# Hyena's inverse transform by even and odd times, around the first tiles of the output product; router and experts asked for apart

## The reference, cut to what matters

```python
p = h @ w_in                                  # 1024 -> 3 * 1024
p = sum(pp[:, j:j + L] * conv_w[j] for j in range(3)) + conv_b
x0, x1, v = jnp.split(p, 3, axis=-1)
z = v * x1
z = irfft(rfft(z, 2L) * rfft(circ, 2L))[:L] + bias * z      # circ: the normed filter, both directions
y = x0 * z
return y @ w_out
# then x = x + g1 * mix; h = modulate(rmsnorm(x)); x = x + g2 * moe(h)
```

## Time and profile before

| | us |
|---|---|
| median of 3 runs (lowest, highest) | 1451.49 (1450.65, 1451.81) |
| the profiled execution | 1451.6 |
| its span, first to last instruction | 1449.8 |
| mean granted TensorE clock | 0.969 |
| TensorE busy (share of the span) | 1308.7 (90%) |
| VectorE busy | 637.7 (44%) |
| ScalarE busy | 297.9 (21%) |

### The profile page before, as it was taken

The page is one execution under the profiler, slowest core; times in us unless marked ns, Lnnn a source line. Parts: engine busy times, 40 slices in busy tenths (PEclk is TensorE's granted clock), DMA queues, the critical chain, the costliest instruction groups (busy, mean ns, idle before and its releaser), DMA issues.

```text
span 1449.8 us, 21846 instructions
## 1 busy us (share of the span) xinstructions
PE 1308.7 (90%) x9044; PEld 684.1 (47%) x9044; DVE 637.7 (44%) x1173; ACT 297.9 (21%) x505; POOL 60.2 (4%) x112
## 2 busy tenths in 40 slices
PE   5999888999999888988997999999999978988888
PEld 1445335864444433433445776874454434433334
DVE  5998862354333313222224788554433322222232
ACT  3227342311111111111112114031111111111110
POOL 0010680000000000000000000000000000000000
PEclk9999999999999999999999999989999999999999
DMA  9673965959999999999999770677999999999996
GB/s 378 242 196 83 168 242 205 410 240 372 421 426 421 428 427 428 429 429 424 426 424 301 296 296 34 280 285 289 371 425 422 422 431 423 430 427 429 425 425 246
DMA packets 52598, 502.76 MB, mean 347 GB/s; under 512 B 9548, under 2 KB 16460, under 8 KB 20044
## 3 DMA queue, kind: packets, MB, share of 16 engines
q1 hardware_dynamic: 51948, 499.18, 85.9%
q10 hardware_dynamic: 544, 2.10, 0.4%
HBM read 496.57 MB, written 4.69 MB: 346 GB/s over the span
## 4 chain that ended last, share of the span: by engine, by line
PE 63%; DMA 27%; DVE 5%; issue 2%; SPq 1%; ACT 1%; DVEq 0%; ACTq 0%
PE ps L743 58%; DMA arena<-in_w_experts 23%; DMA arena<-in_ada_w 4%; PE ps L1061 2%; PE ps L446 2%; SPq L490 1%; DVE arena L2027 1%; ACT arena L1397 1%; DVE arena L2203 0%; PE ps L796 0%; DMA arena<-in_mcst 0%; DVE arena L1867 0%; PE ps L1008 0%; DVE arena L1730 0%; DVE arena L2128 0%
## 5 line engine op out<-in xcount | busy, mean ns | idle before, releaser
L743 PE MATMUL ps<-arena 128*32 128x512 f32 (+10 forms) x8224 | 1225.9, 486 | 120.9 <-issue 48.9
L743 PEld LDWEIGHTS ps<-arena 128*32 128x32 f32 (+5 forms) x8224 | 621.9, 130 | 709.0 <-issue 580.5
L1397 ACT ACTIVATE arena<-ps 128x512 f32<-128x512 f32 (+6 forms) x305 | 168.3, 552 | 923.3 <-PE ps L743 768.1
L1397 ACT ACTIVATE arena<-arena 128x256 f32<-128x256 f32 (+7 forms) x140 | 92.3, 681 | 163.3 <-DVE arena L2088 58.3
L2068 DVE SCALAR_TENSOR_TENSOR arena<-arena,ps 128x256 f32<-128x256 f32 x44 | 21.2, 481 | 232.9 <-ACT arena L1397 232.9
L2086 DVE CAST arena<-ps 128x512 bf16<-128x512 f32 x42 | 29.1, 692 | 165.3 <-PE ps L743 165.3
L2023 DVE COPY arena<-ps 128x512 f32<-128x512 f32 x44 | 30.4, 692 | 126.9 <-PE ps L743 126.9
L2056 DVE TENSOR_TENSOR arena<-arena 128x1024 bf16<-128x1024 f32 x42 | 51.5, 1226 | 37.3 <-ACT arena L1397 37.0
L1061 PE MATMUL ps<-arena 128*128 128x128 f32 x352 | 52.8, 273 | 0.0
L2088 DVE TENSOR_TENSOR arena<-ps,arena 128x1024 f32<-128x1024 f32 x42 | 51.4, 1225 | 1.4
L733 POOL MEMSET arena<- 128x1 f32 x2 | 0.2, 102 | 1196.7 <-PE ps L1061 1196.7
(11 more groups left out here) (230 smaller groups left out, 480.2 us busy)
## 6 DMA issues: line engine op xcount, KB each, us to landing
arena<-in_w_experts SPq DMA_DIRECT2D x76, 3072.0 KB, 20.8
arena<-in_w_experts SPq DMA_DIRECT2D x80, 1024.0 KB, 11.5
arena<-in_w_experts SPq DMA_DIRECT2D x38, 2048.0 KB, 19.5
arena<-in_ada_w SPq DMA_DIRECT2D x40, 1024.0 KB, 6.5
arena<-in_hy_w_in SPq DMA_DIRECT2D x6, 2048.0 KB, 11.6
arena<-in_ada_w SPq DMA_DIRECT2D x4, 2048.0 KB, 21.6
arena<-in_w_shared SPq DMA_DIRECT2D x2, 3072.0 KB, 10.7
arena<-in_hy_w_out SPq DMA_DIRECT2D x1, 4096.0 KB, 12.4
```

The costliest lines, as they stand in the source:

```text
L743: return pe.matmul(out, lhsT, rhs, start=start, stop=stop, skip_group_check=skip)
L1397: return act.activation(out, in_, func, **kw)
```

## The change

The inverse transform is split by time: the table's second half now holds the first half's columns ordered by even, then odd times; VectorE folds the two frequency halves of YR and YS by a sum and a difference first, so that each product has 128 columns and one half of the frequencies to sum over. The output term reads the two halves interleaved. Half 0 of the features goes through inverse transform, output terms and its four k of the output product before half 1's filter product is done. The one-column sums move ahead of the first signal spectrum, the square root ahead of the last projection's eviction, and the first tap of the last short filter from VectorE to ScalarE. On SyncE's queue the shared expert, experts 1 and 2, the router's three loads and expert 0 each get waits of their own.

```diff
@@ -545,11 +545,15 @@
                 for e in experts:
                     load(wring[:, slot_of(e)], A["w_experts"][li, e], f"w_pair{min(e // 2, 1)}")
-            def moe_loads(li):
-                sp.wait_ge(sem("x_mixed"), KD * (li + 1))
+            def router_loads(li):
                 load(rw, A["router_w"][li], "rw_in")
                 load(rt_at(0, NE), A["router_b"][li:li + 1].broadcast_to([P, NE]), "rw_in")
                 load(at(r_mc, NMCST), A["mcst"], "rw_in")
+            def moe_loads(li):
+                sp.wait_ge(sem("x_mixed"), KD * (li + 1))
+                if li == 0:
+                    router_loads(0)
                 first_experts(li, (3, 4))
                 def expert_at(c):
@@ -652,10 +656,15 @@
             sp.wait_ge(sem("hy_proj"), 4)
             sp.wait_ge(sem("hf_ready"), 8)
             load(hyo, A["hy_w_out"], "hyo_in")
+            sp.wait_ge(sem("hy_proj"), 6)
+            load(wring[:, SHARED], A["w_shared"][1], "w_shared")
             sp.wait_ge(sem("filter_mm"), 14 + 1)
+            sp.wait_ge(sem("Y_ready"), 2)
+            first_experts(1, (1, 2))
+            sp.wait_ge(sem("conv_mm"), KD)
+            router_loads(1)
             sp.wait_ge(sem("conv_done"), 6)
-            load(wring[:, SHARED], A["w_shared"][1], "w_shared")
-            first_experts(1, range(3))
+            first_experts(1, (0,))
             moe_loads(1)
             for q in range(4):
                 sp.wait_ge(sem("moe_x"), KD + 2 * (q + 1))
@@ -1316,12 +1325,17 @@
                     last.then_inc(sem("turned_mm"), 1)
             def convolve(c):
                 for j in range(4):
-                    for w, (mat, src) in enumerate((("ic", YR), ("is", YS))):
-                        for k in range(2):
-                            last = mm(ps[:, 2 * (1 - c) + j // 2, (j % 2) * L:(j % 2 + 1) * L], src[:, k, (4 * c + j) * P:(4 * c + j + 1) * P], hcst(mat)[:, k],
-                                      w == 0 and k == 0, w == 1 and k == 1)
+                    for b in range(2):
+                        a = (j % 2) * L + b * P
+                        for w, (mat, src) in enumerate((("ic", YR), ("is", YS))):
+                            last = mm(ps[:, 2 * (1 - c) + j // 2, a:a + P], src[:, b, (4 * c + j) * P:(4 * c + j + 1) * P], hcst(mat)[:, 1, b * P:(b + 1) * P],
+                                      w == 0, w == 1)
                     last.then_inc(sem("conv_mm"), 1)
+            def mixed(j, k):
+                return mm(ps[:, 4 + j // 2, (j % 2) * L:(j % 2 + 1) * L], hyo[:, k, j * P:(j + 1) * P], zt[:, k], j % 2 == 0 and k == 0, k == KD - 1, skip=True)
             for k in range(KD):
                 pe.wait_ge(sem("squared"), 12 + k + 1)
@@ -1359,32 +1373,37 @@
                 halves(4 + 2 * c, "fs", zd, c, "filter_mm")
             pe.wait_ge(sem("z_ready"), 2 + 4)
             project(5, range(0, 1))
+            pe.wait_ge(sem("hf_sums"), 2)
+            for j in range(KD):
+                last = mm(ps[:, 3, j:j + 1], hf[:, 2, j * P:(j + 1) * P], ones[:, 0:1], True, True)
+            last.then_inc(sem("filter_mm"), 1)
             pe.wait_ge(sem("spectrum_read"), 2)
             signal_spectrum(0)
             project(5, range(1, 3))
             pe.wait_ge(sem("spectrum_read"), 3)
             signal_spectrum(1)
             project(5, range(3, 4))
-            pe.wait_ge(sem("hf_sums"), 2)
-            for j in range(KD):
-                last = mm(ps[:, 3, j:j + 1], hf[:, 2, j * P:(j + 1) * P], ones[:, 0:1], True, True)
-            last.then_inc(sem("filter_mm"), 1)
             pe.wait_ge(sem("Y_ready"), 1)
             pe.wait_ge(sem("yh_terms"), KD + 1)
             convolve(0)
+            pe.wait_ge(sem("hyo_in"), 16)
+            pe.wait_ge(sem("spectrum_read"), 4)
+            for k in range(4):
+                pe.wait_ge(sem("yh_ready"), k + 1)
+                for j in range(KD):
+                    mixed(j, k)
             pe.wait_ge(sem("hyp_evicted"), 6)
             pe.wait_ge(sem("Y_ready"), 2)
             convolve(1)
-            pe.wait_ge(sem("hyo_in"), 16)
-            for k in range(4):
+            for k in (4, 5):
                 pe.wait_ge(sem("yh_ready"), k + 1)
                 for j in range(KD):
-                    mm(ps[:, 4 + j // 2, (j % 2) * L:(j % 2 + 1) * L], hyo[:, k, j * P:(j + 1) * P], zt[:, k], j % 2 == 0 and k == 0, False, skip=True)
+                    mixed(j, k)
             for j in range(KD):
-                for k in range(4, KD):
+                for k in (6, 7):
                     if j == 0:
                         pe.wait_ge(sem("yh_ready"), k + 1)
-                    last = mm(ps[:, 4 + j // 2, (j % 2) * L:(j % 2 + 1) * L], hyo[:, k, j * P:(j + 1) * P], zt[:, k], False, k == KD - 1, skip=True)
+                    last = mixed(j, k)
                 last.then_inc(sem("mix_mm"), 1)
             moe_pe(1)
@@ -1638,10 +1657,13 @@
                     for m in range(4):
                         act.wait_ge(sem("Z_mm"), m + 1)
                         ch.then(f(odd_part[m % 2], ps[:, 5 + 2 * (m % 2), :], ACT.Copy), "odd_copied")
-                else:
-                    f(at(r_pad + 2, 1), at(r_eps, 1), ACT.Sqrt)
                     act.wait_ge(sem("filter_mm"), 14 + 1)
                     ch.then(f(hns, ps[:, 3, 0:8], ACT.Sqrt, bias=at(r_eps, 1)), "yh_terms")
+                else:
+                    for j in range(4):
+                        c = 4 * HYP[n] + j
+                        ins = f(short(c), pp[:, n % 2, j], ACT.Identity, scale=col("convw", 24 + c), bias=col("convb", c))
+                        ch(ins) if j < 3 else ch.then(ins, "hyp_evicted")
             moe_act(1)
@@ -2166,29 +2188,46 @@
                     ins = tt(H[:, 1, half], *((even, odd) if w == 0 else (odd, even)), SU)
                     ch(ins) if c == 0 else ch.then(ins, "spectrum_read")
-            def filtered(c):
-                half = slice(c * 512, (c + 1) * 512)
+            def filtered_ends(c):
                 for w, Z in enumerate((ZR, ZS)):
                     dve.wait_ge(sem("odd_copied"), 4 + 2 * c + w + 1)
                     even, odd = ps[:, 4 + 2 * w, :], odd_part[w]
                     ch(tt(Z[:, 0], even, odd, AD))
                     ins = tt(Z[:, 1], *((even, odd) if w == 0 else (odd, even)), SU)
                     ch(ins) if w == 0 else ch.then(ins, "spectrum_read")
-                ch(tt(YR[:, :, half], ZR, HR[:, :, half], M))
-                ch(tt(ytmp, ZS, HS[:, :, half], M))
-                ch(tt(YR[:, :, half], YR[:, :, half], ytmp, SU))
-                ch(tt(YS[:, :, half], ZR, HS[:, :, half], M))
-                ch(tt(ytmp, ZS, HR[:, :, half], M))
-                ch.then(tt(YS[:, :, half], YS[:, :, half], ytmp, AD), "Y_ready")
+            def filtered(c):
+                half = slice(c * 512, (c + 1) * 512)
+                yr_, ys_ = YR[:, :, half], YS[:, :, half]
+                ch(tt(ytmp, ZR, HR[:, :, half], M))
+                ch(tt(yr_, ZS, HS[:, :, half], M))
+                ch(tt(ytmp, ytmp, yr_, SU))
+                ch(tt(yr_[:, 0], ytmp[:, 0], ytmp[:, 1], AD))
+                ch(tt(yr_[:, 1], ytmp[:, 0], ytmp[:, 1], SU))
+                ch(tt(ytmp, ZR, HS[:, :, half], M))
+                ch(tt(ys_, ZS, HR[:, :, half], M))
+                ch(tt(ytmp, ytmp, ys_, AD))
+                ch(tt(ys_[:, 0], ytmp[:, 0], ytmp[:, 1], SU))
+                ch.then(tt(ys_[:, 1], ytmp[:, 0], ytmp[:, 1], AD), "Y_ready")
+            def convolved(j):
+                dve.wait_ge(sem("conv_mm"), j // 2 * 2 + 2)
+                by_time = zt[:, j].rearrange("p (t b) -> p t b", b=2)
+                sums = ps[:, 2 * (1 - j // 4) + j % 4 // 2, (j % 2) * L:(j % 2 + 1) * L].rearrange("p (b t) -> p t b", b=2)
+                ch(stt(by_time, sums, hns[:, j:j + 1], by_time, M, AD))
+                ch.then(tt(zt[:, j], zt[:, j], x0[:, j], M), "yh_ready")
             def short_filters(n):
-                dve.wait_ge(sem("hyp_evicted"), n + 1)
+                dve.wait_ge(sem("hyp_evicted"), n + 1 if n < 5 else n + 2)
                 for j in range(4):
                     c = 4 * HYP[n] + j
                     p_in, o = pp[:, n % 2, j], short(c)
-                    ch(ts(o, p_in, col("convw", 24 + c), col("convb", c), M, AD))
+                    if n < 5:
+                        ch(ts(o, p_in, col("convw", 24 + c), col("convb", c), M, AD))
                     ch(stt(o[:, 1:L], p_in[:, 0:L - 1], col("convw", c), o[:, 1:L], M, AD))
                     ins = stt(o[:, 0:L - 1], p_in[:, 1:L], col("convw", 48 + c), o[:, 0:L - 1], M, AD)
                     ch(ins) if j < 3 else ch.then(ins, "conv_done")
@@ -2214,10 +2253,8 @@
             ch(dve.memset(row_pick[:, 2 * GROUP - 2:2 * GROUP - 1], 1.0))
             modulation_sum(0)
             dve.wait_ge(sem("fw_in"), 16 * 18)
-            for name, odd_sign in (("ic", -1.0), ("is", 1.0)):
```

(19 more changed lines are left out.)

## The result

The changed kernel took 1445.1 us (median of 5 runs, 1440.96 to 1448.37) against 1451.81 of the kernel before on the same chip (1450.65 to 1455.88): ratio 0.9949 [0.993, 0.9969], 6.7 us or 0.5% faster. The forecast was 1441.4 us, with a range from 1438.5 to 1446.0. Two later sets of runs of the same kernel gave medians of 1442.45 us (ratio 0.9933 [0.9908, 0.9957]) and 1442.78 (0.9947 [0.9929, 0.9965]). Its 24 runs together have a median of 1442.77 (1439.0 to 1453.91), 1.4 us above the forecast. Three executions of the kernel before (1580.31, 3430.87 and 3430.96 us) are slow ones and left out of the ratios; the medians include them.

A forecast was written before the change was run, and what follows sets the result against it. TensorE ahead of the full expert stream was taken as the bound: 6.7 width, 1.45 gap and 3.1 clock, less 1.1 new wait and rounding, make 10.1 us, from 1451.49 to 1441.4 us; range 1438.5 to 1446.

The forecast's parts named there:

- The sum: End of Hyena's mix moves from 950.35 to 940.2 us: 10.1 us saved, passed on to the total.
- Width: Inverse transforms on TensorE: 64 instructions fall from 0.216 to 0.111 us with 128 columns, saving 6.7 us.
- Rival 2: Weight loads bound the narrow products at 0.201 us each; mix ends 944.7, total 1446 us; chance 0.03.
- Gap and root: Ahead of the first inverse transform: moving sums and root removes TensorE's 1.45 us wait for ScalarE.
- Clock: TensorE behind that gap: the half clock (1.2 GHz, 6.8 us) disappears, saving 3.1 us.
- VectorE's chain: VectorE from 889.9 to the fifth output term at 926.4 runs without a gap and sets the mix's end.
- The new wait: TensorE, after the second inverse transform at 925.3, waits 1.1 us for the fifth output term.
- rival 1: The 1.1 us wait at 925.3 also drops the clock, costing 3.1 us: total 1444.5; chance 0.13.
- Rival 3: Expert stream starts independently of routing, so the end does not follow the mix: 1451.5 us, no change; chance 0.07.
- x: Extra time per interleaved output-term read on VectorE, counted five times; slower overall from 2.0 us on.
- rival 4: VectorE's strided PSUM reads of output terms make the kernel slower: 1457 us at 2.5 us extra each; chance 0.03.
- The loads: SyncE's earlier router loads costed at nothing; without ScalarE's cover they would give back up to 0.9 us.

The follow-up runs named there:

- split_only: Kernel before with only the even/odd time split, its folded sums and interleaved read; order, first taps and loads as before: median 4.3 us slower, stretch 2.0 longer.
- sums_first: Kernel before with only the one-column sum products and the square root moved earlier: median 2.5 us lower, stretch 3.85 us shorter.
- root_late: Changed kernel with the one-column sum products and the square root back in their old places: stretch 52.95 us, 2.3 longer than with the move.
- loads_only: Kernel before with only the new order of loads on SyncE: median 1450.06 us, 2.0 below the kernel before; stretch 58.88 us.
- term_before_last_taps: Changed kernel with VectorE making the fifth output term ahead of the fourth channel's taps: median 1441.28 us over 12 runs, stretch 49.63 us.
- delay: Changed kernel plus 12 unused products of 512 columns ahead of the first inverse transform: stretch 9.5 us longer, median 10.2 to 10.5 us above the changed kernel's.
- loads_as_before: Changed kernel with SyncE's old order of loads, router's three behind the residual add: median 14.1 us above the changed kernel's; TensorE 15.66 us idle.
- clock_fill: term_before_last_taps plus unused idle products in TensorE's waits at the start of Hyena and at layer 1's routing: median 1443.28 us.

## Why the prediction was right

- **The sum.** 10.1 us were forecast for the stretch and 9.85, 9.83 and 9.82 measured in the three profiles. The experts behind took 490.55, 491.80 and 489.92 against 491.92, inside the 2.2 us that I had allowed. The total came 1.4 us above the forecast over 24 runs. That remainder, like the first median's 3.7 us, is smaller than the range in which executions begin the stretch (889.95 to 896.82 for one and the same code).
- **Width.** 0.111 us was taken for an instruction of 128 columns; in split_only 32 of them took 3.81 us with the end of the last one, 0.119 each, so the term was some 0.25 us too large per convolution, or less by what the last one's end takes. Rival 2, loads of 0.201 us each, would be 6.4 us: excluded.
- **Gap and root.** The gap of 1.45 us went as described. sums_first and root_late price the move from both sides: 3.85 us in the old order, 2.3 in the new one.
- **Clock.** This term was mis-sized in kind. I took 3.1 us as fixed, from one fall in one profile. The same gap cost about 1.5 us less in loads_only and in root_late, and split_only had no half clock behind it. The forecast could use 3.1 because the profile that it was subtracted from had that fall; the four profiles with the old gap give 3.1, 1.5, about 1.4 (2.28 less 1.45 for the gap, with 0.52 added for the shorter wait behind it) and nothing. That the 10.1 fit to 0.3 is therefore in part luck: against 58.88, the stretch of the same computation in loads_only, the change saves 8.2.
- **VectorE's chain.** 36.5 us were reckoned from the ends of half 0 to the fifth term; after, it is done at 933.27, 36.45 behind 896.82. I said this chain would set the end of the mix, and it did until term_before_last_taps took the fifth term out of its way.
- **The new wait.** 1.1 us forecast; 0.81, and 0.29 in root_late and 0.46 in delay. In none of the three did the clock fall behind it as rival 1 has it (1.00 at 932 to 936 after). Its condition, an idle microsecond, was nearly met there, and met in split_only: a wait of 1.61 us ended at 925.55 and the clock stayed at 1.00. Gaps of 1.45 us had a fall in three profiles of four, so the rival did not come true, but it is not shown that a wait of 1.1 us is safe.
- **The end follows.** Rival 3 fell by delay and by every other row of the table but one.
- **The strided read.** The output term's two steps take 0.48 and 0.42 us, those of the earlier trace rows: x is 0, rival 4 falls. The rule on non-contiguous access in "PSUM — Partial Sum Buffer", Specifications, of the Trainium skill speaks of matmuls; for VectorE's read no cost shows.
- **The loads: a condition that I did not work out.** "The router's weights are no longer behind the residual add ... I cost it at nothing; without that cover it would give back up to 0.9." As a difference to the kernel before it is nothing. But under the new computation the old order costs 14 us, as loads_as_before shows, since the change itself moves the taps that release the experts to within 16 us of the mix. The router's early loads are a condition of the gain, larger than the gain. I had worked out that the experts' 12 MB end near 945 and not asked what stands behind them in the queue if nothing is done; with the early issue in_mcst takes 15.2 us to land instead of 4.7. It lands at 948.6, 1.1 us behind the start of the last residual add, and the norm ahead of the router's product at 954.05 hides that.

The parts alone are worth +4.3 (split), -2.5 (sums and root) and -2.0 us (loads, unclear), together about nothing; the change gave 6.7 to 10.2 in its three comparisons. Counted in stretches they are +2.0, -3.85 and, with nothing but another fall of the clock, -1.6, against -9.85. The rest belongs to the order on TensorE and VectorE and to the first tap on ScalarE; neither was tried alone. Without the split TensorE has no wait of over 0.26 us in sums_first for the order to fill, so it should pay only with the split, which is argued and not shown.

## What to carry to other kernels

Price a reordering by the stretch between two marks of unchanged code and check that the next stage keeps its length; the changed kernel's agreed within 0.03 us where the profiled totals differed by 5. That holds while no fall of the clock lies inside: the same computation took 60.50 and 58.88 us. Before costing a small load at nothing, ask what is ahead of it in its queue under the new timing, for whatever releases the big loads may have moved too. A change that takes work off the bounding engine and gives it to another can be slower alone, so try such a split with the order that fills the new wait.

## What the runs showed of the hardware

- The same gap of 1.45 us at the same place came with 6.8 us at 1.2 GHz (before), with 3.3 (loads_only), with full speed for some 1.4 us of work and then about 3.4 us at 1.2 GHz (root_late), or with full speed throughout the 3.81 us of products behind it (split_only).
- Executions of one kernel begin the same late stretch up to 6.9 us apart, partly by falls of the clock at other places (0.62 against 1.00 at 801 to 810 us). What else makes the spread from 1439.0 to 1453.91 stays open; keeping the clock up at two places, as clock_fill did, did not narrow it.
- The half clock at the routing delays the router's product by up to 1.5 us: it starts 6.09 us behind the residual add where the clock falls 5.1 us behind the add, 7.61 where it falls after 2.2. Idle products that held the clock at 1.00 did not gain that back (7.03).
